# Differential attention: the second score product on 64 rows as pairs, with a row's denominators and results made by GpSimd

## The chip, the core and the metric

The kernel runs on one core of one Trainium2 chip. A core has five engines that run side by side and wait for each other through semaphores: TensorE (PE; its weight loads are shown apart as PEld), VectorE (DVE), ScalarE (ACT), GpSimd (POOL) and the engine that issues most transfers (SP). The metric is the device time of one execution in microseconds (us). Before the change it is 3203.32 us, the median of three runs (3199.81 to 3205.28).

## The reference

One layer of a hybrid encoder: 2048 tokens, width 1024, fp32. RMSNorm and one projection give queries, keys and values of two attention groups; their results are projected back, then follow an MLP, a gated embedding and a last norm. The change touches only group A, the differential attention:

```python
def block(qblk):
    s = jnp.einsum('bhmqd,bhmkd->bhmqk', qblk.astype(jnp.float32) * scale, kf)
    pr = jax.nn.softmax(s, axis=-1)
    a = pr[:, :, 0] - lam * pr[:, :, 1]
    return jnp.einsum('bhqk,bhkd->bhqd', a, vf)
...
o = rms_norm(o, subln_g, SUBLN_EPS) * (1.0 - lam_init)
```

There are 4 heads, each with two softmax maps (m) of 64 dimensions and values of 128 dimensions; 2048 queries look at all 2048 keys.

## The kernel before

The program runs in phases: projections, differential attention (prefix `c_` in the names, about 565 to 1160 us), dilated attention (`b_`), output projection (`d_`), MLP (`e_`, `h_`) and gate (`f_`). Products that need fp32 precision are made from a high and a low part of each operand.

**Rows and units.** The differential phase (`differential_phase`) handles 64 rows; a row is 128 queries of one head (`STEPS = HEADS * TILES`), numbered n. The scores of a row are four units of 128 queries by 1024 keys: map 0 and 1, key half 0 and 1. Each unit fills two PSUM banks, and a ring of three such pairs of banks (`RING = 3`) holds the units.

**Operands.** Partitions 0 to 63 of `qs` hold the high part of a query's 64 dimensions, partitions 64 to 127 the low part. `kt_hi` holds the keys' high part in both halves, `kt_lo` the keys' low part in both halves. So a matmul over all 128 partitions with `kt_hi` gives (q_hi + q_lo) k_hi, and one with `kt_lo` gives (q_hi + q_lo) k_lo. `score(n, u)` makes both for each of the two banks (lines 825 and 826).

**The order on TensorE** is written out by hand: in each quarter q of row n it issues the score unit of row n+2, then `turn(n, q)` (four transposes of the combined probabilities, line 833), then `values(n-1, q)` (four products with the values, line 844, each recorded as two matmuls). Before a unit, TensorE waits until ScalarE has taken the exponentials of the unit three before it, since that frees the banks (`pe.wait_ge(S["exp"], U - RING + 1)`).

**VectorE** takes each unit's negated maximum (line 741), joins two of them (748), adds the denominators of a row (755), inverts the second (761), makes the coefficient (766), combines the two maps (774, twice a row) and scales the result of row n-2 (782). **ScalarE** makes the exponentials (698), copies the turned probabilities (706) and the result (712), and sums the squares (719). **GpSimd** makes the small steps of the RMSNorm in `root` (661, 665, 670). All four go through their rows in program order.

**The SP queue** issues the transfers of the phase in `sync_steps`: the queries of four rows at a time, two groups ahead; the result of row n-3; and at n = 20 and n = 36 the keys and values of the head after next (eight transfers of 512 KB and one of 1 MB). From row 50 on, its steps and those of GpSimd stand between the first steps of the dilated phase (`sync_step`, `pool_rest`). The first keys and queries are issued by ScalarE's queue.

## Time and profile before

| | |
|---|---|
| median of three runs | 3203.32 us (3199.81 to 3205.28) |
| span of the profiled execution | 3196.2 us |
| PE busy | 3116.5 us (98% of the span) |
| PEld busy | 2695.4 us (84%) |
| DVE busy | 1809.0 us (57%) |
| ACT busy | 1553.6 us (49%) |
| POOL busy | 1357.8 us (42%) |
| differential phase, first to last score matmul | 564.6 to 1142.3 us |

The span runs from the first to the last instruction. No separate time was taken of the profiled execution: its span is 7.1 us below the median of the runs, which is taken as what lies around it. Busy shares are averages over phases with different limits, so they say which engine has no slack only when they are read in one phase. A matmul's duration reaches from its start to its modelled end and overlaps with the next one; what a matmul costs TensorE is the distance between the starts of two neighbours.

### The profile page before, as it was taken

Reading aid. Unit: us, or ns where it says so; the run is one execution under the profiler, and the core shown is the slowest. Engines: PE = TensorE matmul, PEld = TensorE weight load, DVE = VectorE, ACT = ScalarE, POOL = GpSimd, SP = SyncE. Lnnn points to the kernel's source line nnn. Section 1 sums busy time; section 2 is a strip of 40 time slices with the busy share of each in tenths; the row PEclk is TensorE's granted clock in tenths of the full one; section 3 lists DMA queues with packets and bytes.
Section 4 is the critical chain, followed back from the end, with each engine's and each line's share of the span. In section 5 each row is a group of like instructions: output and inputs, shape, how many; then the busy total and the mean of one; then the engine's idle time right before and its main releaser. Section 6 shows DMA issues by size and latency. Waiting matters only on the chain.

```text
span 3196.2 us, 48937 instructions
## 1 busy us (share of the span) xinstructions
PE 3116.5 (98%) x17504; PEld 2695.4 (84%) x17504; DVE 1809.0 (57%) x3106; ACT 1553.6 (49%) x2824; POOL 1357.8 (42%) x1113
## 2 busy tenths in 40 slices
PE   8999999999999999998999999899999999999998
PEld 8988889788888999997887888787778888887887
DVE  5134343898989966665556666666445545552222
ACT  4011110687888878884235555555553334333332
POOL 2123331011111146771245666666576656665222
PEclk9999999999999999999999999999999999999999
DMA  5234336303031348756754775477696678665221
GB/s 168 99 102 131 119 109 177 88 22 87 22 88 31 81 103 198 166 146 192 239 172 158 253 235 172 148 252 249 201 289 197 198 242 259 197 189 194 75 75 56
DMA packets 467407, 493.43 MB, mean 154 GB/s; under 512 B 84064, under 2 KB 377312, under 8 KB 461920
## 3 DMA queue, kind: packets, MB, share of 16 engines
q1 hardware_dynamic: 463824, 484.02, 49.6%
q10 hardware_dynamic: 3344, 6.29, 0.8%
q8 instruction: 142, 2.33, 0.3%
q14 instruction: 97, 0.79, 0.1%
HBM read 322.05 MB, written 168.17 MB: 153 GB/s over the span
## 4 chain that ended last, share of the span: by engine, by line
PE 80%; DMA 6%; POOL 5%; ACT 4%; issue 2%; DVE 1%; SPq 1%; POOLq 0%; ACTq 0%; DVEq 0%
PE c_pv L844 6%; PE h_acc L136 6%; PE h_acc L137 6%; PE h_acc L138 6%; PE a_acc L136 6%; PE a_acc L137 6%; PE a_acc L138 6%; PE b_pv L984 4%; PE c_scores L825 3%; PE c_scores L826 3%; PE c_turned L833 3%; PE b_scores L1236 3%; DMA e_a<-w_up_dram 3%; PE b_turned L1246 2%; PE f_gate_acc L136 2%
## 5 line engine op out<-in xcount | busy, mean ns | idle before, releaser
L2312 POOL TENSOR_TENSOR h_u_lo<-h_u_raw,h_u_hi 128x512 fp32r<-128x512 f32 x224 | 380.2, 1723 | 205.0 <-ACT h_u_hi L2308 204.8
L136 PE MATMUL h_acc<-h_w_hi,h_u_hi 128*128 128x512 f32 x896 | 349.9, 391 | 4.0 <-POOL h_u_lo L2312 2.6
L137 PE MATMUL h_acc<-h_w_lo,h_u_hi 128*128 128x512 f32 x896 | 349.5, 390 | 0.0
L138 PE MATMUL h_acc<-h_w_hi,h_u_lo 128*128 128x512 f32 x896 | 349.3, 390 | 0.0
L741 DVE TENSOR_REDUCE c_neg_half<-c_scores 128x1 f32<-128x1024 f32 x256 | 312.7, 1222 | 44.5 <-PE c_scores L826 44.4
L136 PE MATMUL e_acc<-e_b_hi,e_a_hi 128*128 128x512 f32 x768 | 303.3, 395 | 22.4 <-ACT e_u L2047 17.4
L2402 DVE TENSOR_TENSOR h_h<-h_acc,h_h 128x512 f32<-128x512 f32 x224 | 153.6, 689 | 300.3 <-PE h_acc L138 300.3
L698 ACT ACTIVATE c_e<-c_scores,c_neg_max 128x1024 f32<-128x1024 f32 x256 | 286.3, 1119 | 68.1 <-DVE c_neg_max L748 68.1
L138 PE MATMUL e_acc<-e_b_hi,e_a_lo 128*128 128x512 f32 x768 | 300.7, 392 | 0.0
L137 PE MATMUL e_acc<-e_b_lo,e_a_hi 128*128 128x512 f32 x768 | 300.6, 391 | 0.0
L844 PE MATMUL c_pv<-c_v,c_at 128*128 128x128 f32 x2048 | 270.3, 275 | 0.4 <-ACT c_o L712 0.4
L844 PEld LDWEIGHTS c_pv<-c_v,c_at 128*128 128x128 f32 x2048 | 248.6, 192 | 0.7 <-ACT c_o L712 0.5
L2308 ACT CAST h_u_hi<-h_u_raw 128x512 fp32r<-128x512 f32 x224 | 127.5, 617 | 228.6 <-DMA h_u_raw<-s_u 228.5
L665 POOL TENSOR_SCALAR c_mean<-c_ssq,c_eps 128x1 f32<-128x1 f32 x64 | 18.5, 289 | 506.1 <-ACT c_o_junk L719 476.3
L825 PE MATMUL c_scores<-c_kt_hi,c_qs 128*128 128x512 f32 x512 | 225.3, 440 | 7.6 <-ACT c_e L698 7.5
L1798 DVE TENSOR_TENSOR e_a_lo<-e_a,e_a_hi 128x512 fp32r<-128x512 f32 x192 | 166.3, 881 | 111.2 <-ACT e_a_hi L1792 106.5
L826 PE MATMUL c_scores<-c_kt_lo,c_qs 128*128 128x512 f32 x512 | 204.7, 400 | 0.0
L331 ACT ACTIVATE a_hl<-a_prod 128x512 fp32r<-128x512 f32 x64 | 40.5, 633 | 335.3 <-POOL a_prod L458 335.3
L136 PEld LDWEIGHTS h_acc<-h_w_hi,h_u_hi 128*128 128x128 f32 x896 | 168.5, 188 | 40.2 <-POOL h_u_lo L2312 5.2
L137 PE MATMUL a_acc<-a_xt_lo,a_w_hi 128*128 128x512 f32 x512 | 199.3, 389 | 0.0
L136 PE MATMUL a_acc<-a_xt_hi,a_w_hi 128*128 128x512 f32 x512 | 199.3, 389 | 0.0
L138 PE MATMUL a_acc<-a_xt_hi,a_w_lo 128*128 128x512 f32 x512 | 199.3, 389 | 0.0
(204 smaller groups left out, 7867.6 us busy)
## 6 DMA issues: line engine op xcount, KB each, us to landing
h_u_raw<-s_u SPq DMA_DIRECT2D x224, 256.0 KB, 3.5
s_u<-e_u SPq DMA_DIRECT2D x192, 256.0 KB, 3.2
s_qkt<-a_hl SPq DMA_DIRECT2D x128, 256.0 KB, 2.8
e_a<-w_up_dram SPq DMA_DIRECT2D x64, 512.0 KB, 4.7
h_w_raw<-s_t SPq DMA_DIRECT2D x32, 1024.0 KB, 7.9
h_w_raw<-w_down_dram SPq DMA_DIRECT2D x24, 1024.0 KB, 7.8
b_kt<-s_qkt SPq DMA_DIRECT2D x64, 256.0 KB, 9.5
e_t<-w_down_dram SPq DMA_DIRECT2D x32, 512.0 KB, 6.0
```

What stands on the lines that cost most here:

```text
L136: nc.tensor.matmul(out, lhs_hi, rhs_hi, start=first, stop=False, skip_group_check=onto)
L137: nc.tensor.matmul(out, lhs_hi, rhs_lo, start=False, stop=False, skip_group_check=onto)
L138: return nc.tensor.matmul(out, lhs_lo, rhs_hi, start=False, stop=last, skip_group_check=onto)
L698: nc.scalar.activation(e[:, n % 2, m, f * HALF:(f + 1) * HALF], bank(n, u), ACT.Exp, bias=neg_max[:, n % 2, m:m + 1], accum_out=sums[:, n ...
L741: nc.vector.tensor_reduce(neg_half[:, m, f:f + 1], bank(n, u), AX.X, ALU.max, negate=True).then_inc(S["halved"], 1)
L825: nc.tensor.matmul(found, queries, kt_hi[h % 2][:, m, cols], start=True, stop=False)
L826: ins = nc.tensor.matmul(found, queries, kt_lo[h % 2][:, m, cols], start=False, stop=True)
L844: ins = nc.tensor.matmul(pv[:, :VD], at[:, s, c], v[h % 2][:, c], start=(c == 0), stop=(c == KT - 1))
L984: ins = nc.tensor.matmul(pv[:, w % 2, s * W1:(s + 1) * W1], et[:, w % 2, s * chunks + c], v[:, BASE[p] + r * CHUNKS[p] + j + c, side:side ...
L1798: self.nc.vector.tensor_tensor(self.a_lo[q][:], raw, self.a_hi[q][:].bitcast(F32), ALU.subtract).then_inc(S["a_made"], 1)
L2312: self.nc.gpsimd.tensor_tensor(self.u_lo[q][s][:], self.u_raw[q][s][:], self.u_hi[q][s][:].bitcast(F32), ALU.subtract).then_inc(self.S["u_ ...
L2402: nc.vector.tensor_tensor(tile, bank[:], tile, ALU.add).then_inc(S["h"], 1)
```

## The change

Three things change in the differential phase.

1. Of the two products of a score, the second one (with `kt_lo`) uses only 64 partitions: q_hi k_lo, without q_lo k_lo. The two banks of a unit take their second product from different halves of the partitions, so that the two matmuls stand side by side on the two halves of the array: bank 0 from partitions 0 to 63 of `qs` and `kt_lo`, bank 1 from partitions 64 to 127. Partitions 64 to 127 of `qs` hold the low part, so a new tile `q_again` holds the high part there. The order within a unit is first, first, second, second.
2. To make room for `q_again`, queries are loaded for two rows instead of four, in six transfers of 64 KB instead of four of 128 KB, and `sync_steps` issues them at every odd n.
3. `denominators` and `result` move from VectorE to GpSimd. The result becomes two instructions there (times rstd, then times gain), and `pool_steps` orders them: the denominators of row n+1, then root and result of row n-2.

```diff
@@ -572,7 +572,7 @@
     HALF = SEQ // 2
     STEPS = HEADS * TILES
     UNITS = tuple((m, f) for m in range(2) for f in range(2))
-    QT = 4 * P
+    QT, HALF_ROWS = 2 * P, HD
     RING = 3
     SPLIT = 50
     with ExitStack() as mem:
@@ -582,6 +582,7 @@
         kt_hi[0], kt_lo[0] = sb("kt_hi0", [P, 2, SEQ], F32R), sb("kt_lo0", [P, 2, SEQ], F32R)
         v[0] = sb("v0", [P, KT, VD])
         qs = sb("qs", [P, 2, 2, QT], F32R)
+        q_again = sb("q_again", [P, 2, 2, QT], F32R)
         kt_hi[1], kt_lo[1] = sb("kt_hi1", [P, 2, SEQ], F32R), sb("kt_lo1", [P, 2, SEQ], F32R)
         v[1] = sb("v1", [P, KT, VD])
         e = sb("e", [P, 2, 2, SEQ])
...
@@ -619,10 +620,14 @@
 
         def load_q(sp, m):
             if m >= 2:
-                sp.wait_ge(S["scored"], 4 * 4 * (m - 1))
+                sp.wait_ge(S["scored"], 4 * 2 * (m - 1))
             for k in range(4):
                 sp.dma_start(qs[32 * k:32 * k + 32, m % 2].bitcast(F32),
-                             rows(0, m // 4, k % 2, k // 2)[:, :, m % 4 * QT:m % 4 * QT + QT]
+                             rows(0, m // 8, k % 2, k // 2)[:, :, m % 8 * QT:m % 8 * QT + QT]
+                             ).then_inc(q_in[m % 2], 16)
+            for k in range(2, 4):
+                sp.dma_start(q_again[32 * k:32 * k + 32, m % 2].bitcast(F32),
+                             rows(0, m // 8, k % 2, 0)[:, :, m % 8 * QT:m % 8 * QT + QT]
                              ).then_inc(q_in[m % 2], 16)
 
...
@@ -646,8 +651,8 @@
 
         def sync_steps(sp, steps):
             for n in steps:
-                if n % 4 == 2 and n // 4 + 2 < STEPS // 4:
-                    load_q(sp, n // 4 + 2)
+                if n % 2 == 1 and (n + 3) // 2 < STEPS // 2:
+                    load_q(sp, (n + 3) // 2)
                 if n >= 3:
...
+        def denominators(pool, n):
+            pool.wait_ge(S["exp"], 4 * n + 4)
+            if n >= 4:
+                pool.wait_ge(S["eps"], n - 3)
+                pool.wait_ge(S["coef"], n - 3)
+            nc.gpsimd.tensor_tensor(den[:, n % 4], sums[:, n % 2, :, 0], sums[:, n % 2, :, 1],
+                                    ALU.add).then_inc(S["den"], 1)
+
+        def result(pool, n):
+            s = n % 2
+            pool.wait_ge(S["rstd"], n + 1)
+            if n >= 2:
+                pool.wait_ge(stored[s], n // 2 * 16)
+            nc.gpsimd.tensor_scalar(out[:, s], o[:, s], rstd[:, s:s + 1], 1.0, ALU.mult, ALU.mult).then_inc(S["scaled"], 1)
+            pool.wait_ge(S["scaled"], n + 1)
+            nc.gpsimd.tensor_tensor(out[:, s], out[:, s], gain[:], ALU.mult).then_inc(S["out"], 1)
+
+        def pool_steps(pool, steps):
+            for n in steps:
+                if n + 1 < STEPS:
+                    denominators(pool, n + 1)
+                if n >= 2:
+                    root(pool, n - 2)
+                    result(pool, n - 2)
+
...
-                def denominators(n):
-                    dve.wait_ge(S["exp"], 4 * n + 4)
-                    if n >= 4:
-                        dve.wait_ge(S["eps"], n - 3)
-                    nc.vector.tensor_tensor(den[:, n % 4], sums[:, n % 2, :, 0], sums[:, n % 2, :, 1],
-                                            ALU.add).then_inc(S["den"], 1)
-
...
-                def result(n):
-                    s = n % 2
-                    dve.wait_ge(S["rstd"], n + 1)
-                    if n >= 2:
-                        dve.wait_ge(stored[s], n // 2 * 16)
-                    nc.vector.scalar_tensor_tensor(out=out[:, s], in0=o[:, s], scalar=rstd[:, s:s + 1],
-                                                   in1=gain[:], op0=ALU.mult, op1=ALU.mult).then_inc(S["out"], 1)
 
...
-                            denominators(n + 1)
                             reciprocal(n + 1)
                             coefficient(n + 1)
                         if q == 2 and 0 <= n + 1 < STEPS:
                             combine(n + 1, 0)
-                        if q == 3 and n >= 2:
-                            result(n - 2)
 
             @block.gpsimd
             def _(pool):
-                for n in range(SPLIT):
-                    root(pool, n)
+                project.wait_constants(pool)
+                pool_steps(pool, range(-1, SPLIT + 2))
 
             @block.tensor
...
                     if u == 0:
-                        pe.wait_ge(q_in[n // 4 % 2], 64 * (n // 8 + 1))
+                        pe.wait_ge(q_in[n // 2 % 2], 96 * (n // 4 + 1))
                     if t == 0 and u == 0:
                         pe.wait_ge(k_in[h % 2], 128 * (h // 2 + 1))
                     if U == 2:
                         project.wait_banks(pe)
                     if U >= RING:
                         pe.wait_ge(S["exp"], U - RING + 1)
-                    queries = qs[:, n // 4 % 2, m, t % 4 * P:t % 4 * P + P]
+                    toks = slice(t % 2 * P, t % 2 * P + P)
+                    cols = [slice(f * HALF + b * 512, f * HALF + b * 512 + 512) for b in range(2)]
+                    found = [scores[:, (U + 1) % RING * 2 + b] for b in range(2)]
                     for b in range(2):
-                        cols = slice(f * HALF + b * 512, f * HALF + b * 512 + 512)
-                        found = scores[:, (U + 1) % RING * 2 + b]
-                        nc.tensor.matmul(found, queries, kt_hi[h % 2][:, m, cols], start=True, stop=False)
-                        ins = nc.tensor.matmul(found, queries, kt_lo[h % 2][:, m, cols], start=False, stop=True)
+                        nc.tensor.matmul(found[b], qs[:, n // 2 % 2, m, toks], kt_hi[h % 2][:, m, cols[b]],
+                                         start=True, stop=False)
+                    for b in range(2):
+                        rows = slice(b * HALF_ROWS, (b + 1) * HALF_ROWS)
+                        ins = nc.tensor.matmul(found[b], (qs, q_again)[b][rows, n // 2 % 2, m, toks],
+                                               kt_lo[h % 2][rows, m, cols[b]], start=False, stop=True)
                     ins.then_inc(S["scored"], 1)
 
...
         def pool_rest(pool):
-            for n in range(SPLIT, STEPS):
-                root(pool, n)
+            pool_steps(pool, range(SPLIT + 2, STEPS + 2))
 
```

The first place is TensorE in the steady part of the phase, from the end of one quarter to the start of the next but one. Before:

```order
L833 MATMUL c_turned<-g_ident,c_a_row 128x128 x4
L844 MATMUL c_pv<-c_v_5435,c_at 128x128 x4
L825 MATMUL c_scores<-c_kt_hi_5437,c_qs 128x512
L826 MATMUL c_scores<-c_kt_lo_5438,c_qs 128x512
L825 MATMUL c_scores<-c_kt_hi_5437,c_qs 128x512
L826 MATMUL c_scores<-c_kt_lo_5438,c_qs 128x512
L833 MATMUL c_turned<-g_ident,c_a_row 128x128 x4
```

The same place in the changed program:

```order
L849 MATMUL c_turned<-g_ident,c_a_row 128x128 x4
L860 MATMUL c_pv<-c_v_5440,c_at 128x128 x4
L837 MATMUL c_scores<-c_kt_hi_5438,c_qs 128x512 x2
L841 MATMUL c_scores<-c_kt_lo_5439,c_qs 128x512
L841 MATMUL c_scores<-c_kt_lo_5439,c_q_again 128x512
L849 MATMUL c_turned<-g_ident,c_a_row 128x128 x4
```

A unit still has four score matmuls; the two with `kt_lo` now follow each other, use 64 rows each, and stand between 128-row matmuls on either side.

The second place is the SP queue where the keys and values of the third head are loaded (step n = 20), with the transfers after them. Before:

```order
L645 DMA s_od<-c_out 128x128 [waits c_out] x3
L633 DMA c_kt_hi_5433<-s_qkt 32x2x2048 [waits c_scored]
L633 DMA c_kt_hi_5433<-s_qkt 32x2x2048 x3
L633 DMA c_kt_lo_5434<-s_qkt 32x2x2048 x4
L639 DMA c_v_5435<-s_vd 128x16x128 [waits c_pv]
L645 DMA s_od<-c_out 128x128 [waits c_out]
L624 DMA c_qs<-s_qkt 32x2x512 [waits c_scored]
L624 DMA c_qs<-s_qkt 32x2x512 x3
```

In the changed program:

```order
L650 DMA s_od<-c_out 128x128 [waits c_out] x2
L638 DMA c_kt_hi_5433<-s_qkt 32x2x2048 [waits c_scored]
L638 DMA c_kt_hi_5433<-s_qkt 32x2x2048 x3
L638 DMA c_kt_lo_5434<-s_qkt 32x2x2048 x4
L644 DMA c_v_5435<-s_vd 128x16x128 [waits c_pv]
L625 DMA c_qs<-s_qkt 32x2x256 [waits c_scored]
L625 DMA c_qs<-s_qkt 32x2x256 x3
L629 DMA c_q_again<-s_qkt 32x2x256 x2
L650 DMA s_od<-c_out 128x128 [waits c_out] x2
```

Before, the first transfer behind the head's load is a result, and the queries behind it are those of rows 28 to 31. Now the first six behind it are the queries of rows 24 and 25.

## Rows read from the trace of the kernel before

**Rows 1.** Busy time by stretch, steady part (busy us, xinstructions; clock; DMA share; GB/s)
```profile
945.00:1035.00 90.00, 90.00 (x638) 80.93 (x637) 81.86 (x121) 73.85 (x150) 10.68 (x30) 1.00 0.07 20
```

**Rows 2.** Timeline of PE, one quarter (start us, us, what)
```profile
1001.22 0.48 PE L825 MATMUL c_scores<-c_kt_hi,c_qs 128*128 128x512 f32 x1
1001.53 0.39 PE L826 MATMUL c_scores<-c_kt_lo,c_qs 128*128 128x512 f32 x1
1001.76 0.39 PE L825 MATMUL c_scores<-c_kt_hi,c_qs 128*128 128x512 f32 x1
...
1002.23 0.60 PE L833 MATMUL c_turned<-g_ident,c_a_row 128*128 128x128 f32 x4
...
1003.47 0.48 PE L825 MATMUL c_scores<-c_kt_hi,c_qs 128*128 128x512 f32 x1
```

**Rows 3.** Timelines of ACT and DVE in a steady row (in brackets: idle before, releaser)
```profile
1002.10 0.20 ACT L698 ACTIVATION_READ_ACCUMULATOR c_e<-c_scores,c_neg_max 128x1 f32 x1
...
1003.84 0.16 DVE L755 TENSOR_TENSOR c_den<-c_sums 128x2 f32<-128x2 f32 x1
...
1004.70 1.23 DVE L741 TENSOR_REDUCE c_neg_half<-c_scores 128x1 f32<-128x1024 f32 x1 [0.19 <-PE c_scores L826]
...
1008.36 0.35 DVE L782 SCALAR_TENSOR_TENSOR c_out<-c_o,c_rstd,g_gain 128x128 f32<-128x128 f32 x1
1009.22 1.22 DVE L741 TENSOR_REDUCE c_neg_half<-c_scores 128x1 f32<-128x1024 f32 x1 [0.51 <-PE c_scores L826]
```

**Rows 4.** Timeline of DVE, third maximum of two early rows
```profile
582.10 1.23 DVE L741 TENSOR_REDUCE c_neg_half<-c_scores 128x1 f32<-128x1024 f32 x1
...
590.13 1.22 DVE L741 TENSOR_REDUCE c_neg_half<-c_scores 128x1 f32<-128x1024 f32 x1
```

**Rows 5.** Timeline of ACT and PE: end of a unit's exponentials, next use of its banks
```profile
1009.66 0.58 ACT L706 COPY c_at<-c_turned 128x512 f32<-128x512 f32 x1
...
1010.27 0.48 PE L825 MATMUL c_scores<-c_kt_hi,c_qs 128*128 128x512 f32 x1
```

**Rows 6.** Largest GpSimd group with 256 elements, groups by line
```profile
L1910 POOL TENSOR_TENSOR e_s<-e_u,e_u 128x256 f32<-128x256 f32 x64 | 66.9, 1046 | 5.0
```

**Rows 7.** Timeline of the SP queue around the third head's load
```profile
762.35 1.84 SPq L633 DMA_DIRECT2D c_kt_hi<-s_qkt  x4
...
771.04 15.15 SPq L645 DMA_DIRECT2D s_od<-c_out  x1
786.23 2.07 SPq L624 DMA_DIRECT2D c_qs<-s_qkt  x4
```

**Rows 8.** Queries behind the first head's load: timeline of ACT's queue, then that transfer's landing
```profile
533.66 20.02 ACTq L624 DMA_DIRECT2D c_qs<-s_qkt  x4
...
DMA to landing us min/median/max: 22.3/22.3/22.3
```

**Rows 9.** Timelines of PE and POOL at the start of row 20
```profile
761.26 0.48 PE L825 MATMUL c_scores<-c_kt_hi,c_qs 128*128 128x512 f32 x1
...
757.51 0.55 POOL L670 TENSOR_TENSOR c_rstd<-c_mean,g_half 128x1 f32<-128x1 f32 x1
```

**Rows 10.** PE after a sparse stretch: timeline, then one stretch with its clock
```profile
1498.74 0.78 PE L136 MATMUL d_acc<-d_wa_hi,d_mt_hi 128*128 128x512 f32 x1
...
1503.15 0.46 PE L137 MATMUL d_acc<-d_wa_lo,d_mt_hi 128*128 128x512 f32 x1
...
1501.00:1503.00 2.00, 2.00 (x6) 1.59 (x5) 1.66 (x5) 0.17 (x1) 0.00 (x0) 0.50 0.81 267
```

**Rows 11.** Busy time by stretch, around the loads of the third and fourth head
```profile
770.00:800.00 30.00, 28.98 (x202) 25.54 (x202) 25.51 (x39) 22.99 (x48) 3.75 (x9) 1.00 0.69 153
915.00:945.00 30.00, 29.46 (x209) 26.36 (x208) 26.35 (x38) 23.31 (x49) 3.20 (x9) 1.00 0.75 163
```

**Rows 12.** Timelines of POOL and PE at the start of the dilated phase
```profile
1174.33 3.77 POOL L1168 CAST b_q<-b_qs 128x2048 fp32r<-128x2048 f32 x1
...
1174.44 0.74 PE L1236 MATMUL b_scores<-b_k,b_q 128*128 128x256 f32 x4
```

More of the change, by code:

```diff
@@ L556, in wait_banks, with wait_constants @@
             pe.wait_ge(v_done, V_UNITS + TILES)
-        def wait_constants(dve):
-            dve.wait_ge(lam_done, 1)
-            dve.wait_ge(gain_done, 1)
+        def wait_constants(eng):
+            eng.wait_ge(lam_done, 1)
+            eng.wait_ge(gain_done, 1)
     return Projected(store_last, wait_qk_stored, wait_all_stored, wait_qk_buffers, wait_products, wait_banks,
@@ L609, in differential_phase @@
         k_in, q_in, stored, v_in = (kit.sem_pair("c_" + s) for s in ("k_in", "q_in", "stored", "v_in"))
-        names = "scored halved negmax exp den rec coef a a_turned at pv o ssq eps mean rstd out"
+        names = "scored halved negmax exp den rec coef a a_turned at pv o ssq eps mean rstd scaled out"
         S = {name: kit.sem("c_" + name) for name in names.split()}
```

## The prediction

> **What bounds the kernel now.** I read the page's busy shares first: TensorE is busy for 98% of the span, so a change counts only by what it does to TensorE's time or to a wait in front of it. Then the busy time of a steady stretch of the phase that is changed [rows 1]: columns in the order PE, PEld, DVE, ACT, POOL. TensorE has no gap at all in 90 us, at a granted clock of 1.00 (the 2.4 GHz level), and VectorE is at 81.86 of 90 us. So TensorE bounds the phase and VectorE stands close behind. The timeline of TensorE shows what a quarter of a row is made of [rows 2]: a score matmul starts 0.23 us after the one before (1001.53 to 1001.76), the first one takes 0.31 us because its weight load cannot hide behind the short value products before it, the transposes start at 1002.23, and the next quarter at 1003.47, so 2.26 us a quarter and 9.05 us a row (1001.22 to 1010.27 over four quarters) [rows 2, 5].
>
> **Step 1, the pairs.** 256 units each lose what the second `kt_lo` matmul cost, if the two 64-row matmuls run side by side: 0.233 us. They also gain two changes between 128-row and 64-row matmuls, one ahead of the pair and one behind it. The trace of before has no 64-row matmul, so this is bounded from both sides. Lower end: a change costs nothing, as in the step from scores to transposes: from 1001.53 to 1002.23 are three starts, 0.233 us each, the last of them the transposes' [rows 2]. Upper end of what I take for likely: TensorE lets the matmul in flight end before it goes on, which is 0.39 us duration less 0.23 us distance, 0.16 us a change [rows 2]. Far end: a change keeps TensorE still for as long as a whole matmul is recorded, 0.39 us. I take 0.05 us for both changes together, because the only change of kind with a price in the trace, 0.08 us into the scores (0.31 against 0.23), comes behind short products that hide no weight load, while the pair stands behind a matmul of 512 columns. So a unit saves s = 0.18 us and a row shrinks from 9.05 to 8.33 us. The first rows of the phase are not bound by TensorE but by the fill (the rows without a wait on VectorE lie there, [rows 4]); I take 13 of the 256 units for that, so the gain is 243 x 0.18 = 43.7 us. The Trainium skill's page "TensorE: Matmul & The Clock Gate", Part 3, says that matmuls on different row groups start about 4 ns apart; no run here shows it, and by it the pair alone would cost 0.004 us more than one matmul.
>
> **Step 2, does VectorE let TensorE have it?** In a steady row VectorE waits 0.19 and 0.51 us for scores [rows 3], so it needs 9.05 - 0.70 = 8.35 us: it would be the bound if nothing moved. An early stretch proves it: two rows in which it never waits are 8.03 us apart, without a result in them [rows 4]. The denominators take 0.16 us and the result 0.35 us [rows 3]; 8.03 - 0.16 gives 7.87 us a row for the changed kernel, 0.46 us below TensorE's 8.33. The second guard is the ring of banks. A unit that starts at 1003.47 has its exponentials done at 1009.66, when ScalarE's next copy starts, and its banks are used again at 1010.27 [rows 2, 5]: 0.61 us of slack in three quarters. With s, three quarters lose 3s and the unit's own way loses s, so the slack is 0.61 - 2s: 0.25 us at s = 0.18, 0.14 us at s = 0.233. It holds, but thinly.
>
> **Step 3, GpSimd's new work.** It does about 1.1 us a row now [rows 1]: 10.68 us in 90 us. Denominators add about 0.3 us and the result two instructions on 128 elements. Each costs between 0.55 us (one element, [rows 9]) and 1.05 us (256 elements, [rows 6]), less for the one with a single tensor; I take 1.1 us for the two, 2.1 at most. That makes 2.5 of 8.3 us. What waits for it: VectorE's reciprocal, with the third maximum queued behind it. ScalarE's last sum of a row is read at 1002.30 and the denominators are made at 1003.84 [rows 3]: 1.5 us, which cover a GpSimd step of 0.3 us. Nothing is charged; if this cover went, each row would lose the difference, up to 0.5 us, 30 us in all. The Trainium skill's "GPSIMD Engine Reference", section 4.1, speaks against such a move, two-input work being about 2 times slower there than on VectorE. Here that changes no sum, since GpSimd is idle for most of a row. At the end of the phase it does cost: the casts for the dilated phase follow the last root, and TensorE's first matmul on them starts at 1174.44, right as GpSimd has gone on to the next casts at 1174.33 [rows 12]. The last result pushes them by 1.1 us: +1.0 us.
>
> **Step 4, the queries behind a head's load.** This is the term that a diff does not show. The transfer behind the nine transfers of a head is held at its issue: before, that is a result, 15.15 us, until 786.19 or 23.8 us after the first key transfer (762.35) [rows 7]. With queries in that place, in the first head's load, the four issues took 20.02 us and the first landed 22.3 us after its issue [rows 8], so about 3.8 us after it was let go. In the changed kernel the first transfers behind the load are the queries of rows 24 and 25 (and of 40 and 41), which TensorE needs at the start of row 22. The load starts when the result of row 17 is stored. Row 20 starts at 761.26 (its first score matmul); rstd of row 17 is ready at 758.06 [rows 9]; plus 1.1 us for GpSimd's result and 0.4 us for the store, the load starts 1.7 us before row 20. Held for 23.8 us, five more issues at 0.5 us (2.07 us for four, [rows 7]), 3.0 us to land, as they are half as large: 29.3 us after the load's start, 27.6 us after row 20's. Row 22 wants to start 2 x 8.33 = 16.7 us after row 20's. So TensorE stands still for 10.9 us. After an idle stretch the granted clock is 0.50, the 1.2 GHz level: from 1498.74 to 1503.15 ten matmuls took 4.4 us instead of 2.3, until the clock rose [rows 10], 2.1 us lost; I add 0.5 us for the other engines' refill. 13.5 us, twice: +27.0 us. What goes are the stalls of before at the same place, where VectorE's result waited for its store: 1.02 and 0.54 us of TensorE [rows 11], -1.6 us; GpSimd takes that wait now, under the new one. The other loads of queries have two rows and no such load ahead; they cost nothing, except that rows 4 and 5 at the start come within 1 us of their need.
>
> **Sum.** -43.7 + 27.0 - 1.6 + 1.0 = -17.3 us. Against the profiled span of 3196.2 us that is 3178.9; with the 7.1 us between that span and the median of the runs, **3186 us** (-0.5%).
>
> **Rivals.**
> - *Full overlap, free changes* (s = 0.233): 243 x 0.233 = 56.6 gained, row 8.12, each stall 27.6 - 16.2 + 2.6 = 14.0: -56.6 + 28.0 - 0.6 = -29.2, **3174 us**. For it: the change to transposes is free in the trace. Against: those are not of another height.
> - *No stall at the loads* (s = 0.18): -43.7 - 0.6 = -44.3, **3159 us**. It needs queries that pass the loads; both rows of before show that they do not.
> - *No overlap*: four matmuls at 0.23 us each as before, s = 0, stall 27.6 - 18.1 + 2.6 = 12.1 twice, -0.6: +23.6, **3227 us**. The edit then does not do what it says.
> - *The other side: every change of height empties the array.* Place: ahead of and behind each pair. Price: 0.16 us a change, s = 0.233 - 0.32 = -0.09, +22 us over 256 units; row 9.41, stall 27.6 - 18.8 + 2.6 = 11.4 twice, -0.6: +44.2, **3248 us**. It decides from s below 0.10: there 243s no longer pays for the stalls (-243s + 2(12.1 + 8s) - 0.6 = 0). The Trainium skill's "TensorEngine Tiling (Array Packing)", Key Properties, says that changing the tiling mode drains TensorE, without a time; that is this rival, and no row here speaks to it.
> - *A whole matmul's length a change*, 0.39 us: s = -0.55, +140, row 11.2, stalls 7.8 twice, -0.6: +155, **3358 us**.
>
> **Chances.** Forecast 0.30, full overlap 0.17, no stall 0.08, no overlap 0.12, emptied array 0.25, whole matmul 0.08. Change of more than 0.2% (6.4 us) is what a measurement of this kernel can tell from none. Faster: 0.17 + 0.08 + 0.26 of the forecast's 0.30 = 0.51; same 0.07 (the rest of the forecast and a part of the no-overlap case); slower 0.42. The forecast's own range is 3176 to 3198 us. For 8 in 10 the range reaches over no stall and over the emptied array: **3154 to 3252 us**; left out are the whole matmul a change and the edges.
>
> **What would show it.** Pairs: the two 64-row matmuls start within a few hundredths of a microsecond, and the transposes about 0.83 us after a quarter's first score (1.01 before); starts 0.23 us apart mean no overlap, and a first 64-row matmul 0.39 us or more behind the one before means emptying. VectorE: rows of about 8.3 us with short waits for scores; no waits at all at 7.8 us would make it the bound. GpSimd: the reciprocal never waits for the denominators. Loads: one pause of TensorE of about 10 us near 770 us and one near 905 us, ending when queries land, with the clock at 0.50 behind them. I am wrong if the row is not between 8.1 and 8.5 us or if those pauses are missing.

## The result: slower by 1.6%

The changed kernel takes 3251.68 us (median of four runs, 3248.63 to 3253.87), the kernel before took 3201.57 us beside it (four runs, 3194.79 to 3205.28). The ratio is 1.0159, with a 95% interval from 1.0147 to 1.0171. The forecast was 3186 us, so the difference has the wrong sign. The profiled execution took 3248.63 us with a span of 3246.8 us, so 1.8 us lie around a span, not the 7.1 us that were taken for it. Between the two profiled spans lie 50.6 us (3246.8 less 3196.2).

Busy time of a stretch that no pause touches, beside [rows 1]; columns as there:

```profile
820.00:910.00 90.00, 90.00 (x607) 66.93 (x606) 74.59 (x93) 70.30 (x143) 19.46 (x56) 1.00 0.10 29
```

TensorE is still full at a granted clock of 1.00, but makes 607 matmuls in 90 us where it made 638. VectorE fell from 81.86 to 74.59 us; TensorE got none of it. A quarter of a row on TensorE, the counterpart of [rows 2] (start us, us, what):

```profile
862.45 0.71 PE L837 MATMUL c_scores<-c_kt_hi,c_qs 128*128 128x512 f32 x2
863.09 0.49 PE L841 MATMUL c_scores<-c_kt_lo,c_qs 64*128 64x512 f32 x1
863.09 0.50 PE L841 MATMUL c_scores<-c_kt_lo,c_q_again 64*128 64x512 f32 x1
863.52 0.66 PE L849 MATMUL c_turned<-g_ident,c_a_row 128*128 128x128 f32 x4
864.01 1.06 PE L860 MATMUL c_pv<-c_v,c_at 128*128 128x128 f32 x8
864.83 0.71 PE L837 MATMUL c_scores<-c_kt_hi,c_qs 128*128 128x512 f32 x2
```

The two 64-row matmuls start together (863.09), so the overlap is real. Yet the quarter takes 2.38 us (862.45 to 864.83) against 2.26, and the transposes start 1.07 us after the quarter, against 1.01. The weight loads of the same quarter show where the time is:

```profile
863.09 0.18 PEld L841 LDWEIGHTS c_scores<-c_kt_lo,c_qs 64*128 64x128 f32 x1 [0.37 <-issue]
863.09 0.18 PEld L841 LDWEIGHTS c_scores<-c_kt_lo,c_q_again 64*128 64x128 f32 x1
863.52 0.42 PEld L849 LDWEIGHTS c_turned<-g_ident,c_a_row 128*128 128x128 f32 x4 [0.24 <-issue]
```

Both loads at a change of height start with the very matmul that needs them. TensorE's waits of the phase (waits view, 560 to 1220 us: us in total, times, longest):

```profile
DVE c_neg_half L771 <- PE c_scores L841: 118.0, 131, 10.7
PEld c_scores L841 <- issue: 95.0, 256, 0.7
...
PEld c_turned L849 <- issue: 61.3, 248, 0.7
...
PE c_scores L837 <- DMA c_q_again<-s_qkt: 16.2, 2, 8.7
...
DVE c_rec L784 <- POOL c_den L682: 2.1, 1, 2.1
```

The load waits for "issue" in each of the 256 units ahead of the pair and in nearly each behind it. The two pauses for queries are there too. Here they are on TensorE, and below it the first of them on the SP queue, the counterpart of [rows 7]:

```profile
797.76 1.22 PE L837 MATMUL c_scores<-c_kt_hi,c_qs 128*128 128x512 f32 x2 [8.65 <-DMA c_q_again<-s_qkt]
...
802.11 1.20 PE L837 MATMUL c_scores<-c_kt_hi,c_qs 128*128 128x512 f32 x2
...
805.33 0.71 PE L837 MATMUL c_scores<-c_kt_hi,c_qs 128*128 128x512 f32 x2
...
960.69 1.22 PE L837 MATMUL c_scores<-c_kt_hi,c_qs 128*128 128x512 f32 x2 [7.56 <-DMA c_q_again<-s_qkt]
...
964.81 0.71 PE L837 MATMUL c_scores<-c_kt_hi,c_qs 128*128 128x512 f32 x2
```

```profile
767.83 1.84 SPq L638 DMA_DIRECT2D c_kt_hi<-s_qkt  x4
...
772.53 20.66 SPq L625 DMA_DIRECT2D c_qs<-s_qkt  x4
793.23 1.08 SPq L629 DMA_DIRECT2D c_q_again<-s_qkt  x2
```

Behind the head's nine transfers the queries were held at their issue for 20.66 us. After the first pause two quarters took 7.57 us (797.76 to 805.33) in place of 4.75, the first two matmuls 1.22 us instead of 0.71: 2.8 us more, at a mean granted clock of 0.58. After the second one only one quarter was slow, 4.12 us (960.69 to 964.81) in place of 2.38, at 0.55: 1.7 us more.

The 50.6 us, from the two traces: a row is 9.52 us in the stretch shown (four quarters from 862.45 to 871.97) and 9.47 later (1002.70 to 1012.17). Over the 237 undisturbed quarters of the trace, from the start of one unit's scores to the next, the mean is 2.375 us, so 9.50 us a row, against 2.264 and 9.05 before. Over the 243 units that the forecast counted this is 243 x 0.111 = 27.0; the two pauses 16.2; the clock behind them 2.8 + 1.7 = 4.5; stalls of before that are gone -1.6. These four make 46.1 us, and from the first to the last score matmul the phase grew by 45.8 (577.7 us before, 623.5 now, 564.4 to 1187.9). The start of the dilated phase adds 3.8, told below. The sum is 49.9 us; 0.7 us are not placed.

### The profile page after: what moved, and what is told of

It reads as the page before. It is cut to its first block, busy times and chain, and to the rows that moved or that the text cites. A ratio compares the mean times of both kernels' runs of the same rounds, so it can differ in the third digit from the quotient of the medians.

```text
span 3246.8 us, 49130 instructions
## 1 busy us (share of the span) xinstructions
PE 3145.5 (97%) x17504; PEld 2627.1 (81%) x17504; DVE 1789.0 (55%) x2978; ACT 1554.9 (48%) x2824; POOL 1425.4 (44%) x1305
## 4 chain that ended last, share of the span: by engine, by line
PE 81%; POOL 5%; DMA 5%; ACT 4%; issue 2%; SPq 1%; DVE 1%; POOLq 0%; ACTq 0%; DVEq 0%
PE c_pv L860 7%; PE h_acc L136 6%; PE h_acc L138 6%; PE h_acc L137 6%; PE a_acc L138 5%; PE a_acc L137 5%; PE a_acc L136 5%; PE c_turned L849 5%; PE b_pv L999 4%; PE c_scores L837 4%; PE c_scores L841 3%; PE b_scores L1251 3%; DMA e_a<-w_up_dram 3%; PE b_turned L1261 2%; PE e_acc L136 2%
## 5 line engine op out<-in xcount | busy, mean ns | idle before, releaser
L736 ACT COPY c_at<-c_turned 128x512 f32<-128x512 f32 x256 | 150.1, 586 | 133.9 <-PE c_turned L849 127.6
L682 POOL TENSOR_TENSOR c_den<-c_sums 128x2 f32<-128x2 f32 x64 | 12.5, 195 | 450.2 <-ACT c_e L728 450.2
L837 PE MATMUL c_scores<-c_kt_hi,c_qs 128*128 128x512 f32 x512 | 185.4, 444 | 21.5 <-DMA c_q_again<-s_qkt 16.2
```

The costliest lines, as they stand in the source:

```text
L736: nc.scalar.copy(at[:, n % 2, 4 * g:4 * g + 4].rearrange("p c t -> p (c t)"), turned[:]).then_inc(S["at"], 1)
L837: nc.tensor.matmul(found[b], qs[:, n // 2 % 2, m, toks], kt_hi[h % 2][:, m, cols[b]], start=True, stop=False)
```

## The experiments

Each kernel is compared with the kernel before, run on the same chip. "Before" medians lie between 3199.0 and 3201.8 us.

### Queries of two rows alone

```diff
-    QT = 4 * P
+    QT = 2 * P
-                if n % 4 == 2 and n // 4 + 2 < STEPS // 4:
-                    load_q(sp, n // 4 + 2)
+                if n % 2 == 1 and (n + 3) // 2 < STEPS // 2:
+                    load_q(sp, (n + 3) // 2)
```

> The kernel before with one part of the change: queries are loaded for two rows instead of four (four transfers of 64 KB, at every odd n); products of 128 rows and VectorE's work as before. Theory A (queries behind a head's load stall TensorE): two pauses before rows 22 and 38. The load starts 1.1 us after row 20 here, is held 23.8 us, three more issues 1.5 us, 3 us to land, so 29.4 us against two rows of 9.05 us: 11.3 us of pause and about 2.8 us of low clock behind it, less the 1.6 us of the old stalls: +27 us, ratio 1.008. Theory B (the extra time comes from the pairs alone): no pause, within 2 us of before.

Measured: 3225.34 us, ratio 1.0081 (1.0068 to 1.0095). TensorE waits for queries twice, 21.2 us, and the first pause is

```profile
790.99 0.79 PE L825 MATMUL c_scores<-c_kt_hi,c_qs 128*128 128x512 f32 x1 [10.86 <-DMA c_qs<-s_qkt]
```

So the smaller groups of queries are enough to make the pauses. Among the kernels with six transfers a group the first pause is longer the shorter a row is: 5.5 us at a row of 10.43 us, 8.65 at 9.50, 9.4 and 9.7 at 9.05, and 10.2 at 8.57.

### GpSimd's new work alone

The kernel before, with `denominators` and `result` on GpSimd, as in the change, and nothing else of it:

```diff
-                for n in range(SPLIT):
-                    root(pool, n)
+                project.wait_constants(pool)
+                pool_steps(pool, range(-1, SPLIT + 2))
```

> The kernel before with only the move of denominators and result to GpSimd; 128-row products and groups of four rows as before, but the two matmuls with kt_hi and kt_lo of each bank as before. Theory A: rows stay at 9.05 us since TensorE bounds them; the stalls of 1.6 us at the loads go, TensorE's wait for the casts at the start of the dilated phase grows by up to 4 us: +0 to +3 us, ratio 1.000 to 1.001. Theory C (GpSimd's reads disturb VectorE or ScalarE, or its denominators come late): rows longer than 9.05 us, +10 us or more.

Measured: 3200.94 us, ratio 1.0005 (0.9996 to 1.0014): no cost that can be told. What moved at the start of the dilated phase, TensorE here, and then the same second use of `b_k` in the kernel before:

```profile
1172.86 1.22 PE L1244 MATMUL b_scores<-b_k,b_q 128*128 128x256 f32 x4 [3.92 <-POOL b_k L1179]
...
1179.50 0.70 PE L1244 MATMUL b_scores<-b_k,b_q 128*128 128x256 f32 x4
```

```profile
1177.97 0.72 PE L1236 MATMUL b_scores<-b_k,b_q 128*128 128x256 f32 x4
```

Counted from TensorE's first dilated scores (1157.70 here, 1160.24 before), GpSimd has these casts done 0.9 us later, which is what the forecast had (1.0). But TensorE comes for them 3 us earlier, because here it waits 1.0 us for exponentials ahead of them instead of 2.4 and has no stretch at a low clock there (0.66 before, from 1164 to 1169). So it now waits 3.9 us where it waited for nothing, and behind that wait the two steps from 1172.86 to 1179.50 take 6.64 us in place of 3.53 (1174.44 to 1177.97 before): 3.1 us of low clock. In the changed kernel the same stretch lasts 21.56 us (1206.02 to 1227.58) against 17.73 before (1160.24 to 1177.97), so the price there is 3.8 us.

### The head's load one step later

```diff
-                if n % TILES == 4 and n >= TILES and n // TILES + 1 < HEADS:
+                if n % TILES == 5 and n >= TILES and n // TILES + 1 < HEADS:
```

> The changed kernel with the head's load one step later on the SP queue (n = 21 and 37), behind the queries of rows 24 and 25 and a store. Theory A: both pauses go (8.7 and 7.5 us) with 2.8 us of low clock each, so 20 to 22 us faster than the changed kernel, about 3230 us, ratio to before 1.009; rows stay at 9.47 us. Rival: the stall only moves to the next group (rows 26 and 27, needed two rows later): then less than 8 us are won.

Measured: 3232.62 us, ratio 1.0105 (1.0092 to 1.0119), without any wait of TensorE for queries. That is 19 us under the changed kernel's 3251.68: most of the pauses with their clock (16.2 + 4.5 us), given back by one number. The quarters stay at 2.38 us.

### The second product on 128 rows again

```diff
-                        rows = slice(b * HALF_ROWS, (b + 1) * HALF_ROWS)
-                        ins = nc.tensor.matmul(found[b], (qs, q_again)[b][rows, n // 2 % 2, m, toks],
-                                               kt_lo[h % 2][rows, m, cols[b]], start=False, stop=True)
+                        ins = nc.tensor.matmul(found[b], qs[:, n // 2 % 2, m, toks], kt_lo[h % 2][:, m, cols[b]],
+                                               start=False, stop=True)
```

> The changed kernel with only the pairs undone: the second product on 128 rows, in the order kt_hi, kt_lo, kt_hi, kt_lo; small groups with six transfers, q_again loaded but not read, GpSimd's work stay. Theory A (changes between 64 and 128 rows cost more than the pair saves): rows back at 9.05 us, 26 us won; pauses of 9.5 us and 2.8 us of low clock remain, so about 3227 us, ratio 1.008. Theory D (the pairs are not what lengthens the row): rows stay near 9.4 us and the time near 3250 us.

Measured: 3228.79 us, ratio 1.0094 (1.0079 to 1.011), 23 us under the changed kernel although its pauses are 2 us longer (18.2 us). Four matmuls cost less than two and a pair.

### The same in the changed kernel's order

```diff
+                    for kt, last in ((kt_hi, False), (kt_lo, True)):
+                        for b in range(2):
+                            ins = nc.tensor.matmul(found[b], qs[:, n // 2 % 2, m, toks],
+                                                   kt[h % 2][:, m, cols[b]], start=not last, stop=last)
```

> The changed kernel with four 128-row matmuls in the new order kt_hi, kt_hi, kt_lo, kt_lo. Control for the order of banks: theory A expects 0.233 us from start to start and rows of 9.05 us, 3229 us like the kernel with the pairs undone. If the alternation of the banks or of the key tiles costs something, the row is longer than 9.05 us.

Measured: 3224.63 us, ratio 1.0068 (1.0048 to 1.0088). The order costs nothing. This kernel has the changed kernel's sequence without a change of height, so its quarter is the one to compare with, matmuls and then loads:

```profile
862.55 0.71 PE L838 MATMUL c_scores<-c_kt_hi,c_qs 128*128 128x512 f32 x2
863.10 0.62 PE L838 MATMUL c_scores<-c_kt_lo,c_qs 128*128 128x512 f32 x2
863.57 0.60 PE L846 MATMUL c_turned<-g_ident,c_a_row 128*128 128x128 f32 x4
864.00 1.06 PE L857 MATMUL c_pv<-c_v,c_at 128*128 128x128 f32 x8
864.81 0.71 PE L838 MATMUL c_scores<-c_kt_hi,c_qs 128*128 128x512 f32 x2
```

```profile
862.87 0.42 PEld L838 LDWEIGHTS c_scores<-c_kt_lo,c_qs 128*128 128x128 f32 x2
863.34 0.59 PEld L846 LDWEIGHTS c_turned<-g_ident,c_a_row 128*128 128x128 f32 x4
```

Here each load stands 0.23 us ahead of its matmul (862.87 and 863.10, 863.34 and 863.57). From the quarter's start to the second product are 0.55 us, in the changed kernel 0.64: **0.09 us more ahead of the pair**. From there to the transposes 0.47 against 0.43, where 0.233 had gone: **0.19 us more behind the pair's start**. From the transposes to the values 0.43 against 0.49: **0.06 us more**. Together 0.34 us a unit against the 0.233 saved.

### Both 64-row matmuls on the same rows

```diff
-                        rows = slice(b * HALF_ROWS, (b + 1) * HALF_ROWS)
-                        ins = nc.tensor.matmul(found[b], (qs, q_again)[b][rows, n // 2 % 2, m, toks],
+                        rows = slice(0, HALF_ROWS)
+                        ins = nc.tensor.matmul(found[b], qs[rows, n // 2 % 2, m, toks],
```

> The changed kernel, but both 64-row matmuls of a unit use partitions 0 to 63 (the same half of the array). Same products, same two changes of height, no partner side by side. If the pair in the changed kernel really overlaps, each unit gets 0.23 us longer: quarter 2.60 instead of 2.37 us, row 10.4 us, +60 us less some 8 us of pause, about 3303 us. If the overlap were only in the records, the time would stay near 3251 us.

Measured: 3317.97 us, ratio 1.0359 (1.0339 to 1.038); the quarter grows by 0.23 us to 2.61. The time is 15 us above the forecast. Some 10 of them lie in the phase: among its first rows two quarters took 4.76 and 4.75 us (593.68 to 603.19) at a granted clock of 0.50, where the changed kernel had 1.00. The rest lies outside the phase and is not explained. The quarter decides between the two theories: the overlap is worth the whole 0.233 us, and the price of the changes, 0.34 us a unit, is the same when both matmuls use one half of the array.

### The pair first

The pair stands ahead of the two matmuls on 128 rows, so behind the values of the quarter before:

```diff
-                        nc.tensor.matmul(found[b], qs[:, n // 2 % 2, m, toks], kt_hi[h % 2][:, m, cols[b]],
-                                         start=True, stop=False)
-                    for b in range(2):
...
+                    for b in range(2):
+                        ins = nc.tensor.matmul(found[b], qs[:, n // 2 % 2, m, toks], kt_hi[h % 2][:, m, cols[b]],
+                                               start=False, stop=True)
```

> The changed kernel with the pair ahead of the two 128-row score matmuls instead of behind them; same products, two changes of height a unit, now value products -> pair -> scores of 128 rows. Theory E (at a change the next matmul waits until the one in flight has streamed and about 0.11 us more, then its weight load of 0.10 us is exposed): the first change falls where a load was exposed anyway (0.08 us), so unit 1.03 instead of 1.12 us, quarter 2.29, row 9.15, 64 x 0.32 = 20 us faster, about 3231 us. Theory F (a change costs a fixed time wherever it stands): quarter 2.37 and 3251 us as the changed kernel.

Measured: 3259.64 us, ratio 1.0177 (1.0162 to 1.0192). The theory that such a move would save had forecast 3231 us and falls; the fixed price (3251 us) is nearer, and is too low as well. The quarter:

```profile
862.05 0.49 PE L838 MATMUL c_scores<-c_kt_lo,c_qs 64*128 64x512 f32 x1
862.06 0.50 PE L838 MATMUL c_scores<-c_kt_lo,c_q_again 64*128 64x512 f32 x1
862.49 0.73 PE L841 MATMUL c_scores<-c_kt_hi,c_qs 128*128 128x512 f32 x2
863.05 0.60 PE L849 MATMUL c_turned<-g_ident,c_a_row 128*128 128x128 f32 x4
863.48 1.06 PE L860 MATMUL c_pv<-c_v,c_at 128*128 128x128 f32 x8
864.47 0.50 PE L838 MATMUL c_scores<-c_kt_lo,c_qs 64*128 64x512 f32 x1
```

From the values to the pair are 0.99 us (863.48 to 864.47) where 0.81 led to a 128-row score: a change behind the short products costs 0.17 us, more than the 0.09 behind 512 columns. The transposes are back at 0.60 us, since no change precedes them. The price moved with the change, and for both changes it is 0.39 us here (a quarter of 2.42 against 2.26, and 0.233 saved).

### Both products as pairs

```diff
+                    for kt, last in ((kt_hi, False), (kt_lo, True)):
+                        for b in range(2):
+                            rows = slice(b * HALF_ROWS, (b + 1) * HALF_ROWS)
+                            ins = nc.tensor.matmul(found[b], (qs, q_again)[b][rows, n // 2 % 2, m, toks],
+                                                   kt[h % 2][rows, m, cols[b]], start=not last, stop=last)
```

> The changed kernel with the first product as a pair too: both with 64 rows, q_hi k_hi and q_hi k_lo. It leaves out q_lo k_hi. Still two changes of height a unit, none between the two pairs, one place in a row fewer for matmuls. Theory E: pair to pair 0.31 us (a load exposed) and no more, unit 0.76 us with its changes, quarter 2.01, row 8.05 us, where the ring of banks and VectorE come close: 64 x 1.4 = 90 us faster less some 5 us of longer pauses, about 3166 us. If each 64-row matmul were slow by itself (0.42 us from pair to transposes), pair to pair would be 0.42 us, row 8.5 us, about 3195 us.

Measured: 3199.89 us, ratio 0.9988 (0.9979 to 0.9998), 34 us above the first case and near the 3195 of the second. The quarter is 2.14 us:

```profile
860.91 0.49 PE L839 MATMUL c_scores<-c_kt_hi,c_qs 64*128 64x512 f32 x1
860.91 0.49 PE L839 MATMUL c_scores<-c_kt_hi,c_q_again 64*128 64x512 f32 x1
861.25 0.39 PE L839 MATMUL c_scores<-c_kt_lo,c_qs 64*128 64x512 f32 x1
861.25 0.39 PE L839 MATMUL c_scores<-c_kt_lo,c_q_again 64*128 64x512 f32 x1
861.57 0.66 PE L847 MATMUL c_turned<-g_ident,c_a_row 128*128 128x128 f32 x4
```

Two pairs save 0.466 us and one change on each side costs 0.35, so the quarter falls by 0.12. But the distance between the pairs, 0.34 us, left two readings: the first pair's uncovered load, or pairs that are slow by themselves. The next kernel tells them apart.

### The pair twice

The later load, and

```diff
-                    for b in range(2):
-                        rows = slice(b * HALF_ROWS, (b + 1) * HALF_ROWS)
-                        ins = nc.tensor.matmul(found[b], (qs, q_again)[b][rows, n // 2 % 2, m, toks],
-                                               kt_lo[h % 2][rows, m, cols[b]], start=False, stop=True)
+                    for last in (False, True):
+                        for b in range(2):
+                            rows = slice(b * HALF_ROWS, (b + 1) * HALF_ROWS)
+                            ins = nc.tensor.matmul(found[b], (qs, q_again)[b][rows, n // 2 % 2, m, toks],
+                                                   kt_lo[h % 2][rows, m, cols[b]], start=False, stop=last)
```

> The changed kernel with a head's load one step later (3232.6 us, quarter 2.38 us), and the pair of 64-row matmuls issued twice in every unit, so that the second product is added twice. Theory C (the price lies at the change between 128 and 64 rows, on either side: 0.09 us for the switch plus 0.10 and 0.06 us for the weight load that comes after it instead of ahead): a further pair has no change of its own and costs what a matmul costs, 0.233 us, quarter 2.61 us, 256 x 0.233 = +60, so 3292 us (ratio to the kernel before 1.029), and the load of the second pair stands ahead of the first pair's end. Theory D (a pair of 64-row matmuls is slow by itself, 0.34 to 0.43 us each): quarter 2.72 to 2.81, 3320 to 3343 us.

Measured: 3284.8 us, ratio 1.0268 (1.0248 to 1.0289), 52 us over the same kernel with one pair; theory C had 60, for all 256 units. The quarter is 2.60 us where C had 2.61, and 2.72 is ruled out. The second pair's load stands ahead of it:

```profile
860.42 0.18 PEld L842 LDWEIGHTS c_scores<-c_kt_lo,c_qs 64*128 64x128 f32 x1 [0.37 <-issue]
860.42 0.18 PEld L842 LDWEIGHTS c_scores<-c_kt_lo,c_q_again 64*128 64x128 f32 x1
860.53 0.19 PEld L842 LDWEIGHTS c_scores<-c_kt_lo,c_qs 64*128 64x128 f32 x1
```

Its matmuls start at 860.75, 0.22 us after that load. A second pair costs 0.22 us (2.60 less 2.38), like a 128-row matmul; the price lies at the change.

### The later load with 128 rows, and with pairs alone

The kernels "the second product on 128 rows again" and "both products as pairs", each with the later load's one-line edit (`n % TILES == 5`).

> The changed kernel with a head's load one step later and the second product on all 128 rows again. What is left of the change are the queries of two rows, their six transfers and GpSimd's denominators and results. If pairs and pauses are all that the change costs, apart from the casts at the end of the phase (3.9 us), this is the kernel before plus 2 to 4 us less the 1.6 us of its old stalls: 3203 us (ratio 1.0005), quarters of 2.26 us and no wait of TensorE for queries. Rival: the smaller and more numerous transfers cost something of their own in each row or at the loads: 3210 us or more.

Measured: 3203.25 us, ratio 1.001 (1.0001 to 1.002): nothing of the change is left but some 3 us, about the price at the start of the dilated phase. The smaller transfers cost nothing once the head's load stands behind them.

> Both products of a score as pairs of 64-row matmuls (leaves out q_lo k_hi), and a head's load one step later. The same without the later load took 3199.9 us with 20.7 us of TensorE's waits for queries and the lower clock behind them. Theory C: the quarters stay at 2.14 us (one change ahead of the two pairs, one behind, 0.36 us in all, against 0.47 us saved), the waits go: 3199.9 - 20.7 - 5 = 3174 us, ratio 0.992. Rival: at rows of 8.6 us VectorE or the ring of banks takes a part of it, with waits of TensorE for exponentials: 3182 us or more.

Measured: 3179.3 us, ratio 0.9937 (0.9922 to 0.9952), between the theory's 3174 and the rival's 3182. The waits for queries went from 20.7 to 1.5 us; 7.8 us of waits for exponentials stay.

### Without the second product

The kernel with GpSimd's new work, and in a unit

```diff
-                        nc.tensor.matmul(found[b], qs[:, n // 4 % 2, m, toks], kt_hi[h % 2][:, m, cols[b]],
-                                         start=True, stop=False)
-                        ins = nc.tensor.matmul(found[b], qs[:, n // 4 % 2, m, toks], kt_lo[h % 2][:, m, cols[b]],
-                                               start=False, stop=True)
+                        ins = nc.tensor.matmul(found[b], qs[:, n // 4 % 2, m, toks], kt_hi[h % 2][:, m, cols[b]],
+                                               start=True, stop=True)
```

> The kernel before with the denominators and results on GpSimd (3200.9 us), without the second product of a score (leaves out the keys' low part; its loads stay). TensorE would need 9.05 - 4 x 0.466 = 7.19 us a row. This tries the term of the prediction that the real change never reached: VectorE's 7.87 us a row. If it holds: no wait of VectorE for scores, rows of 7.87 us, 61 x 1.18 = -72 us, about +8 us of stalls where results are held behind a head's load: 3137 us (ratio 0.980). Rival: the ring of three pairs of banks is late first, with waits of TensorE for exponentials while VectorE still has short waits for scores: rows of 8.2 us or more, 3157 us or more (0.986).

Measured: 3123.97 us, ratio 0.9769 (0.9755 to 0.9784), 13 us better than expected. Its steady stretch, then the same maximum of two rows on VectorE:

```profile
945.00:1035.00 90.00, 87.51 (x650) 76.49 (x649) 88.39 (x116) 82.00 (x175) 37.38 (x78) 1.00 0.32 83
```

```profile
863.40 1.22 DVE L766 TENSOR_REDUCE c_neg_half<-c_scores 128x1 f32<-128x1024 f32 x1
...
871.10 1.22 DVE L766 TENSOR_REDUCE c_neg_half<-c_scores 128x1 f32<-128x1024 f32 x1
```

VectorE is the bound, at 7.70 us a row, and waits for scores only 2.5 us in the whole phase. This kernel and the last one with pairs alone beat the kernel before, but they make the scores from fewer products than it does.

## Why the prediction was wrong, step by step

**Step 1, the pairs: the step that failed.** The overlap was right, to the hundredth. The price of the two changes was taken at 0.05 us and is 0.34, so s is -0.11 instead of 0.18, and the term is +27.0 instead of -43.7 us. That is off by 71 us, where forecast and result are 66 apart; what is left nearly cancels. The value leaned on the nearest row, the free step from scores to transposes, and that row was of one height on both sides. It did not speak to the change at all, as the text itself said. What it showed was the benefit of a load pulled ahead by 0.23 us; that is just what a change of height takes away. The better clue stood in the same group and was set aside: 0.08 us into the scores was the price of a load with no cover. The runs give the price in parts: 0.09 us for the change itself (0.17 behind short products), 0.10 us for the pair's uncovered load, then 0.09 and 0.06 us for the same on the way back. The 0.10 is what two pairs in a row stand apart over 0.233 (860.42 to 860.75 in the kernel with the pair twice). With the 0.17 from the kernel with the pair first, and 0.03 for a pair's uncovered load over that of a first score (0.34 against 0.31, the 0.34 read in the kernel with pairs alone itself), the parts give 2.26 - 0.466 + 0.17 + 0.03 + 0.09 + 0.06 = 2.14 us for pairs alone; measured are 2.14. How TensorE comes to hold back the load is not in the traces. The sign that the forecast named for emptying, 0.39 us or more from the matmul before to the first 64-row one, did not come: that distance is 0.33 us (median of 256), although the price did. The Trainium skill's "TensorEngine Tiling (Array Packing)", Key Properties, says that changing the tiling mode drains TensorE. The rows agree with it as far as they go: a price at every change of height, 0.34 us for two. The Trainium skill's "TensorE: Matmul & The Clock Gate", Part 3, has matmuls on different row groups start about 4 ns apart; pairs here start 0.00 to 0.01 us apart, which agrees.

**Step 2, VectorE.** Never put to the test in the changed kernel, where TensorE is full. The kernel without the second product reaches it: 7.70 us a row against 7.87, so it was a fair bound on the safe side. The ring of banks did not bind either: at s = 0.466 it had a slack of 0.61 - 0.93, below zero, yet TensorE's waits for exponentials came to 21.1 us in all, and VectorE was the bound.

**Step 3, GpSimd.** Right for the rows. The denominators take 0.19 us and the two result instructions 0.83 (1.1 forecast), and VectorE waits for denominators once:

```profile
1003.86 0.19 POOL L682 TENSOR_TENSOR c_den<-c_sums 128x2 f32<-128x2 f32 x1 [5.90 <-ACT c_e L728]
...
1006.50 0.37 POOL L690 TENSOR_SCALAR c_out<-c_o,c_rstd 128x128 f32<-128x128 f32 x1
1006.96 0.46 POOL L692 TENSOR_TENSOR c_out<-c_out,g_gain 128x128 f32<-128x128 f32 x1
```

At the end of the phase the casts were put off by 0.9 us, as forecast, but the price was 3.8 us in place of 1.0. The term left out that a wait of TensorE there is followed by a low clock (0.54 from 1221 to 1228 us), and that TensorE would come earlier.

**Step 4, the queries behind a head's load.** Right in place, number and size. From the load's first transfer to TensorE's start behind it 29.3 us were forecast, and 29.9 were measured (767.83 to 797.76). The emptied-array rival put the pauses at 27.6 - 18.8 = 8.8 us; 8.65 and about 7.5 were measured. At a row of 9.05 the same sum gives 9.5 us, and the kernels with such rows show 10.86 and 9.4. The clock behind a pause cost 2.8 us once and 1.7 once, where 2.1 and 0.5 for a refill were taken.

**The rival that came true** is the emptied array: 3248 us forecast, 3251.68 measured, a row of 9.41 forecast, 9.50 measured. Its price of 0.16 a change, from the length of a matmul in flight, was near the 0.17 found on average, but it is not made as that text had it: about half of it stands ahead of the load, and half is the load itself. So the closeness is in part luck: between the spans it had 44.2 us where 50.6 were measured. And its chance, 0.25, was too low against a forecast whose own value rested on no row with a change in it.

## What to carry to other kernels

Before a matmul is halved in height, count the changes of height and not the matmuls: here a stretch of shorter matmuls costs 0.34 to 0.39 us for its two ends, by what stands ahead of it, and saves 0.23 us a pair, so it pays from two pairs in a row on. When a change makes TensorE wait where it did not, count the low clock behind the wait too: here 1.7 to 3.1 us for waits of 3.9 to 8.65 us. When one part of a kernel's change shortens the lead of a transfer, look for the large load ahead of it in the same queue; moving that load by one step gave back 19 us. Where the trace lacks the very thing that the edit adds, the nearest row is no value for it, only an end of the range.

## What the hardware showed unexpectedly

A change between 128-row and 64-row matmuls takes away the load that TensorE otherwise pulls 0.23 us ahead. In all kernels with pairs the load of the first pair behind a change starts with its matmul, and that matmul is recorded at 0.49 us instead of 0.39; a second pair in a row has its load 0.22 to 0.23 us ahead and 0.39 us again.

GpSimd's product with the gain took 0.46 us in the changed kernel (median 458 ns, 455 to 463 over all 64). Without the second product its mean was 1.33 us over 59:

```profile
L687 POOL TENSOR_TENSOR c_out<-c_out,g_gain 128x128 f32<-128x128 f32 x59 | 78.6, 1333 | 4.9
```

In the shorter row it starts at 866.36 us, beside VectorE's combination of two maps (866.24 to 867.52), and lasts 1.48 us; in the longer row it starts at 1006.96 beside a maximum. The traces sort it out over the whole phase. Without the second product, the 52 products with the gain that start inside a combination take 1.30 to 1.48 us, and the other 12 take 0.45 to 0.47. In the kernel with both products as pairs, the only one of 64 that starts inside a combination takes 1.50 us. The median combination takes 1.28 us in both the changed kernel and the one without the second product. So GpSimd's two-input product is held up when it starts behind VectorE's two-input one; why is not in the traces.
